# Choosing two experts with VectorE's eight-largest search, with two accumulator sums and one weight step moved on TensorE

## What is computed

```python
g_logits = xt @ w_router_group + b_router_group            # 4 groups
grp = argmax(g_logits); g_w = softmax(g_logits)[grp]
e_logits = (xt @ w_router_expert + b_router_expert).reshape(N, 4, 8)[grp]
top_p, top_i = top_k(softmax(e_logits), 2)
gates = g_w * top_p / sum(top_p)
expert = grp * 8 + top_i
# each chosen expert e, for its tokens: (silu(gate) * up) @ w_down[e], gate, up = split(x @ w_gate_up[e])
out[token] += y * gate
```

## Time and profile before

| | us |
|---|---|
| median of 3 runs | 666.59 |
| lowest and highest | 665.27, 667.97 |
| profiled execution, its own time | 664.23 |
| its span in the profile | 662.4 |
| TensorE busy | 507.2 (77%) |
| VectorE busy | 235.0 (35%) |
| ScalarE busy | 181.7 (27%) |
| read from HBM | 236.50 MB, 359 GB/s over the span |

### The profile page before, as it was taken

The page is one execution under the profiler, slowest core; times in us unless marked ns, Lnnn a source line. Parts: engine busy times, 40 slices in busy tenths (PEclk is TensorE's granted clock), DMA queues, the critical chain, the costliest instruction groups (busy, mean ns, idle before and its releaser), DMA issues.

```text
span 662.4 us, 13304 instructions
## 1 busy us (share of the span) xinstructions
PE 507.2 (77%) x5802; PEld 370.9 (56%) x5802; DVE 235.0 (35%) x522; ACT 181.7 (27%) x399; POOL 20.8 (3%) x21
## 2 busy tenths in 40 slices
PE   3999999999999898885755864765586476558665
PEld 3988998789888655553433532343353234335433
DVE  3796897664644632321111221121121112112203
ACT  6559567264442112110100020010002101000203
POOL 2000111200000000000000000000000000000000
PEclk9999999999999999999877988798798879889978
DMA  8755834396579889999999999999999999999992
GB/s 348 294 187 190 319 145 162 135 398 240 189 278 368 341 350 426 427 447 429 428 425 428 431 433 445 433 433 430 427 427 433 430 439 442 430 410 429 428 414 103
DMA packets 15717, 238.09 MB, mean 359 GB/s; under 512 B 1728, under 2 KB 1856, under 8 KB 3008
## 3 DMA queue, kind: packets, MB, share of 16 engines
q1 hardware_dynamic: 15536, 237.03, 85.9%
q10 hardware_dynamic: 144, 0.52, 0.2%
HBM read 236.50 MB, written 1.05 MB: 359 GB/s over the span
## 4 chain that ended last, share of the span: by engine, by line
PE 48%; DMA 44%; DVE 3%; ACT 2%; issue 1%; another core or an unknown queue 1%; POOL 1%; SPq 0%; POOLq 0%; ACTq 0%; DVEq 0%
DMA ring<-in_w_expert 43%; PE psum L617 15%; PE psum L600 11%; PE psum L903 10%; PE psum L934 4%; DMA landing<-in_dense 1%; PE psum L774 1%; PE psum L751 1%; PE psum L583 1%; PE psum L862 1%; PE psum L927 1%; PE psum L875 1%; POOL stat L1344 1%; PE psum L646 1%
## 5 line engine op out<-in xcount | busy, mean ns | idle before, releaser
L903 PE MATMUL psum<-ring,xg 128*32 128x256 f32 x2048 | 153.4, 461 | 90.4 <-DMA ring<-in_w_expert 84.2
L903 PEld LDWEIGHTS psum<-ring,xg 128*32 128x32 f32 x2048 | 74.3, 131 | 157.0 <-DMA ring<-in_w_expert 90.0
L617 PE MATMUL psum<-split_w,split_act 128*128 128x512 f32 x432 | 101.9, 393 | 1.2 <-DVE res L1596 1.2
L617 PEld LDWEIGHTS psum<-split_w,split_act 128*128 128x128 f32 x432 | 80.3, 188 | 18.3 <-DVE res L1596 1.6
L1282 ACT ACTIVATE small<-psum 128x128 f32<-128x128 f32 x32 | 8.9, 278 | 283.0 <-PE psum L903 283.0
L1839 DVE SCALAR_TENSOR_TENSOR small<-small,psum 128x128 f32<-128x128 f32 x32 | 9.2, 288 | 203.1 <-ACT small L1282 203.1
L1408 DVE TENSOR_TENSOR split_w<-landing,split_w 128x2048 fp32r<-128x2048 f32 x29 | 66.2, 2289 | 30.9 <-ACT split_w L1079 30.8
L1079 ACT ACTIVATE split_w<-landing 128x2048 fp32r<-128x2048 f32 x30 | 57.3, 1915 | 49.3 <-PE psum L617 26.0
L600 PE MATMUL psum<-split_act,split_w 128*128 128x256 f32 x576 | 70.1, 284 | 0.9 <-DVE split_act L1421 0.9
L600 PEld LDWEIGHTS psum<-split_act,split_w 128*128 128x128 f32 x576 | 69.5, 192 | 1.7 <-DVE split_w L1442 1.3
L1850 DVE COPY ybuf<-psum 32x128 f32<-32x128 f32 x128 | 37.3, 291 | 75.5 <-PE psum L934 74.6
(11 more groups left out here) (184 smaller groups left out, 355.4 us busy)
## 6 DMA issues: line engine op xcount, KB each, us to landing
ring<-in_w_expert SPq DMA_DIRECT2D x20, 6144.0 KB, 48.2
ring<-in_w_expert SPq DMA_DIRECT2D x23, 2048.0 KB, 33.8
landing<-in_dense SPq DMA_DIRECT2D x30, 1024.0 KB, 5.5
ring<-in_w_expert SPq DMA_DIRECT2D x26, 1024.0 KB, 8.3
res<-in_x SPq DMA_DIRECT2D x2, 512.0 KB, 3.7
work<-in_mem SPq DMA_DIRECT2D x1, 1024.0 KB, 11.4
ybuf<-in_late SPq DMA_DIRECT2D x1, 512.0 KB, 14.1
after_routing<-in_norm_final SPq DMA_DIRECT2D x1, 512.0 KB, 10.7
```

The source lines that it names most:

```text
L617: i = mm(b, tokens_of(src[t], k0 + k, h), w[a][:, k, :], start=first and k == 0 and n == 0, stop=last and k == CT - 1 and n == 2)
L903: i = mm(half[SLOTS * strip:SLOTS * strip + SLOTS], xg[:, CT * part + k, SLOTS * j:SLOTS * j + SLOTS], w[:, k, :, P * strip:P * strip + P] ...
```

## The change

- choose(h) takes the eight largest of the groups' logits (`V.max`) and their positions (`V.max_index`), masks the other groups' experts, and does the same once over the 32 masked expert logits; the first two positions are compared with 0 to 31 in one operation, whose two rows are added into `picked`. The group logits are padded from 4 to 8 columns with a bias of -1e30, so that a routing matmul has 40 columns. ScalarE's second exponential waits for `expert_arg` and has 2 columns.
- first_slots goes; find_slots and slots_times_rstd, each over all 128 slots, stand in its place. Ahead of the gathered tokens the gates take five linked steps, where there were five and an unlinked one.
- On TensorE, weights 28 are used for half 1 between Tf1 and Tf2; route(0, 1) goes ahead of route(1, 0).
- open_sum(0, 1) and open_sum(1, 1) stand ahead of and behind the last matmul of rank1; group 0 has none any more.

```diff
@@ -76,7 +77,8 @@
                      ("b_ig", CT), ("lru_lambda", CT), ("conv_w", CONV * CT)):
     PARAMS[_name] = (sum(n for _, n in PARAMS.values()), _cols)
 N_PARAMS = sum(n for _, n in PARAMS.values())
-N_ROUTES = GROUPS + EXPERTS
+EIGHT = 8
+N_ROUTES = EIGHT + EXPERTS
 
 
 CONSTS = {}
@@ -147,8 +149,11 @@
 def lay_out_late(inputs):
 
 
-    router = np.concatenate([np.asarray(inputs["w_router_group"])[0], np.asarray(inputs["w_router_expert"])[0]], axis=1)
-    bias = np.concatenate([np.asarray(inputs["b_router_group"]), np.asarray(inputs["b_router_expert"])], axis=1)
+    router = np.zeros((D, N_ROUTES), np.float32)
+    bias = np.full((1, N_ROUTES), -BIG, np.float32)
+    for name, a, n in (("group", 0, GROUPS), ("expert", EIGHT, EXPERTS)):
+        router[:, a:a + n] = np.asarray(inputs[f"w_router_{name}"])[0]
+        bias[:, a:a + n] = np.asarray(inputs[f"b_router_{name}"])
     blocks = np.zeros((P, 2, CT, P), np.float32)
     for n, name in enumerate(("w_rg", "w_ig")):
         w = np.asarray(inputs[name])[0]
...
@@ -803,16 +808,16 @@
             for c in (0, 1):
                 await_read(pe, f"xo{c}")
             turn("Tf", res, (0, 1))
+            tokens(28, ["xo2", "xo3"], os_, 0, last=False, halves=(1,))
             await_read(pe, "xo2")
             turn_late("Tf2", 0, range(CT, KC))
             pe.wait_ge(router_loaded, 16)
             for c in (0, 1):
                 await_read(pe, f"Tf{c}")
             route(0, 0)
-            route(1, 0)
             await_read(pe, "Tf2")
             route(0, 1)
-            tokens(28, ["xo2", "xo3"], os_, 0, last=False, halves=(1,))
+            route(1, 0)
             tokens(29, ["xo2", "xo3"], os_, CT, first=False, halves=(1,))
 
             picked = rt(4)
@@ -842,8 +847,11 @@
             pe.wait_ge(first_taken, 1)
             for part in range(2):
                 gather_first(0, part, range(CT))
+            pe.wait_ge(late_sumsq, 2 * NH)
+            open_sum(0, 1)
             pe.wait_ge(chosen, 2)
             end(mm(pb("rank1")[:, 0:EXPERTS], const("before"), picked[:, 1], start=False, stop=True), "rank1")
+            open_sum(1, 1)
             def count_all():
 
                 for h in range(NH):
...
@@ -978,14 +986,9 @@
                 for h in range(NH):
                     await_read(pe, f"route{h}")
                 gate_up(0, 0, 0, rest_and_count)
-                pe.wait_ge(late_sumsq, 2 * NH)
-                open_sum(0, 1)
                 await_read(pe, "over")
                 finish_expert(0, 0, 0)
-                gate_up(0, 1, 0)
-                open_sum(1, 1)
-                finish_expert(0, 1, 0)
-                for j in range(2, BATCH):
+                for j in range(1, BATCH):
                     expert(0, j, 0)
                 for cb in range(2):
                     scatter(0, cb, range(NH))
...
@@ -1271,8 +1274,8 @@
             release(i, "Tf3")
             act.wait_ge(group_arg, 2)
             nc.scalar.activation(rt(9, GROUPS), rt(8, GROUPS), ACT.Exp).then_inc(group_exp, 1)
-            act.wait_ge(chosen, 2)
-            nc.scalar.activation(soft[:, 32:40], soft[:, 24:32], ACT.Exp).then_inc(expert_exp, 1)
+            act.wait_ge(expert_arg, 2)
+            nc.scalar.activation(soft[:, 32:34], soft[:, 24:26], ACT.Exp).then_inc(expert_exp, 1)
...
@@ -1686,58 +1689,36 @@
             late_mean(0)
 
             def by_group(ap):
...
-            def first_of_max(*searches):
-
-                def operate(stage, src, best, cand, index, pick):
...
+                return ap.rearrange("p (g e) -> p g e", g=GROUPS)
+
+            def eights(n):
+                return small[:, 960 + 16 * n:976 + 16 * n].rearrange("p (h n) -> p h n", h=NH)
+
+            g_sum, less, e21 = soft[:, 52:54], soft[:, 24:26], soft[:, 32:34]
+            gate12 = soft[:, 36:40].rearrange("p (h n) -> p h n", h=NH)
+            g_best, g_index, best, index = eights(0), eights(1).bitcast(U32), eights(2), eights(3).bitcast(U32)
+            other = rt(10, GROUPS)
+            pick12 = small[:, 384:512].rearrange("p (h n e) -> p h n e", h=NH, n=2)
+            picked, masked = rt(4), rt(5)
 
             def choose(h):
 
-                t = slice(h, h + 1)
                 take_logits(h)
-                first_of_max((by_group(e_logit[:, t]), best1[:, t], cand[:, t], index[:, t], pick1[:, t]),
-                             (g_logit[:, t], g_best[:, t], g_cand[:, t], g_index[:, t], g_pick[:, t]))
-                V.tensor_tensor(rt(8, GROUPS)[:, t], g_logit[:, t], spread(g_best[:, t], g_logit[:, t]), ALU.subtract
+                g_logit, e_logit = logit[:, h, 0:EIGHT], by_group(logit[:, h, EIGHT:])
+                link(V.max(g_best[:, h], g_logit))
+                link(V.max_index(g_index[:, h], g_best[:, h], g_logit))
+                link(V.tensor_tensor(other[:, h], iota[:, 0:GROUPS], g_index[:, h, 0:1].to_broadcast([P, GROUPS]), ALU.not_equal))
+                link(V.scalar_tensor_tensor(by_group(masked[:, h]),
+                                            other[:, h].unsqueeze(2).to_broadcast([P, GROUPS, PER_GROUP]), -BIG, e_logit,
+                                            ALU.mult, ALU.add))
+                link(V.max(best[:, h], masked[:, h]))
+                link(V.max_index(index[:, h], best[:, h], masked[:, h]))
+                link(V.tensor_tensor(pick12[:, h], iota[:, 0:EXPERTS].unsqueeze(1).to_broadcast([P, 2, EXPERTS]),
+                                     index[:, h, 0:2].unsqueeze(2).to_broadcast([P, 2, EXPERTS]), ALU.is_equal))
+                V.tensor_tensor(picked[:, h], pick12[:, h, 0], pick12[:, h, 1], ALU.add).then_inc(chosen, 1)
+                V.tensor_tensor(rt(8, GROUPS)[:, h], g_logit[:, 0:GROUPS], g_best[:, h, 0:1].to_broadcast([P, GROUPS]), ALU.subtract
                                 ).then_inc(group_arg, 1)
-                link(V.scalar_tensor_tensor(rt(5)[:, t], rt(2)[:, t], -BIG, e_logit[:, t], ALU.mult, ALU.add))
-                first_of_max((rest[:, t], best2[:, t], cand[:, t], index[:, t], pick2[:, t]))
-                V.tensor_tensor(less[:, t], best2[:, t], best1[:, t], ALU.subtract)
-                link(V.tensor_tensor(picked[:, t], pick1[:, t], pick2[:, t], ALU.add))
-                V.tensor_tensor(picked[:, t], picked[:, t], spread(g_pick[:, t], picked[:, t]), ALU.mult).then_inc(chosen, 1)
+                V.tensor_tensor(less[:, h:h + 1], best[:, h, 1:2], best[:, h, 0:1], ALU.subtract).then_inc(expert_arg, 1)
                 dve.wait_ge(chosen, h + 1)
 
             def place(h):
@@ -1769,24 +1750,18 @@
                     i = slots_times_rstd(h)
                 i.then_inc(taken, 1)
 
-            def first_slots(h):
-
-                for e in range(BATCH):
-                    i = V.tensor_scalar(ntake[:, h, SLOTS * e:SLOTS * e + SLOTS], iota[:, 1:SLOTS + 1],
-                                        rankm[:, h, e:e + 1], stat[:, RS + 6 + h:RS + 7 + h], ALU.is_equal, ALU.mult)
-                return i
-
             choose(0)
             add_xo("xo3", 1, 1)
             late_tokens("Tf4", 6, 2, 1)
             late_mean(1)
             place(0)
-            first_slots(0).then_inc(first_taken, 1)
-            find_slots(0, 0)
+            link(find_slots(0, 0))
+            slots_times_rstd(0).then_inc(first_taken, 1)
             choose(1)
             place(1)
-            first_slots(1).then_inc(taken, 1)
             find_slots(1, 0).then_inc(slots_found, 1)
+            dve.wait_ge(slots_found, 1)
+            slots_times_rstd(1).then_inc(taken, 1)
 
             def give_gates(g):
 
@@ -1813,14 +1788,12 @@
             dve.wait_ge(group_exp, 1)
             link(V.tensor_reduce(g_sum, rt(9, GROUPS), AX.X, ALU.add))
             dve.wait_ge(expert_exp, 1)
-            link(V.scalar_tensor_tensor(gate1, e21, 1.0, spread(g_sum, gate1), ALU.add, ALU.mult))
-            link(V.reciprocal(gate1, gate1))
-            link(V.tensor_tensor(gate1, gate1, g_pick, ALU.mult))
-            link(V.tensor_tensor(e21, e21, gate1, ALU.mult))
-            V.tensor_tensor(pick1, pick1, spread(gate1, pick1), ALU.mult)
+            link(V.scalar_tensor_tensor(g_sum, e21, 1.0, g_sum, ALU.add, ALU.mult))
+            link(V.reciprocal(gate12[:, :, 0], g_sum))
+            link(V.tensor_tensor(gate12[:, :, 1], gate12[:, :, 0], e21, ALU.mult))
+            link(V.tensor_tensor(pick12, pick12, gate12.unsqueeze(3).to_broadcast([P, NH, 2, EXPERTS]), ALU.mult))
             take_gathered(0, 0)
-            link(V.tensor_tensor(pick2, pick2, spread(e21, pick2), ALU.mult))
-            link(V.tensor_tensor(by_group(gates), pick1, pick2, ALU.add))
+            link(V.tensor_tensor(gates, pick12[:, :, 0], pick12[:, :, 1], ALU.add))
             dve.wait_ge(slots_found, 1)
             give_gates(0)
             take_gathered(0, 1)
```

More of the change, by code:

```diff
@@ L20 @@
 I32 = mybir.dt.int32
+U32 = mybir.dt.uint32
 ALU = mybir.AluOpType
@@ L329, in rt @@
```

(4 more changed lines are left out.)

## The result

| | us |
|---|---|
| changed kernel, median of 6 runs | 660.81 (659.99 to 661.90) |
| before, median of 6 runs beside them | 666.11 (665.27 to 667.97) |
| ratio | 0.9933, 95% interval [0.9912, 0.9953] |
| a second set, 8 runs against 31 of before | 0.9952, [0.9931, 0.9973] |
| profiled execution | 660.75, span 658.9 |

The changed kernel is faster by the ratio, by 4.5 us (3.1 to 5.9) in the first set and 3.2 us (1.8 to 4.6) in the second; 2.9 us was forecast. The ratio is not the quotient of the medians: these lie 5.3 us apart in the first set and 2.4 us (664.36 and 661.94) in the second. The two profiled executions are 3.48 us apart.

What follows compares the result with a forecast made beforehand. The weight stream bounds the kernel, its end hanging on when the ring's refill begins. The terms 0.66 + 0.52 + 0.37 + 0.46 + 0.89 = 2.90 us give 666.59 - 2.9 = 663.7 us; range 661.6 to 666.2.

Steps and rivals of the forecast that it cites:

- the prediction's own condition: Weight stream: a sooner end of expert 0's first gate_up half brings the end sooner if the stream is emptied by then.
- (1): TensorE, weights 28's second half ahead of Tf2 and routing: gain 0.66 us; unit 3's earlier load alone gives nothing.
- (2): VectorE's slots of half 0, find_slots and one multiply: only 0.15 us gained, take_logits(1) at 224.5.
- (3): VectorE's search: choose(1) takes 2.15 us instead of 3.45, a search 0.25, `chosen` at 226.7.
- (4): Sums in TensorE's waits: open_sum(0,1) takes 0.94 us, rank1 at 227.6 instead of 228.75, 0.87 of choose(1)'s saving unused.
- (5): VectorE's slots of half 1: 0.37 us less, gather at 228.9, gain 1.55 us so far.
- (6): TensorE's clock does not drop: gate_up begins at 230.8 (0.46 us more), takes 1.93, not 2.82 (0.89 more).
- (7): Router: 40 columns instead of 36, the larger table and the smaller exponential cost nothing.
- A: Rival: TensorE's clock drops all the same, gain only 1.7 us, 664.9; chance 0.16.
- B: Rival: both holes of the weight stream close, the stream never waits, gain 4.3 us, 662.3; chance 0.12.
- C: Rival: VectorE's searches are expensive; at 1.14 us a search the kernel is 0.5% slower, 670; chance 0.04.
- D: Rival: the change does not reach the end, stream's rate or tail moves by as much, 666.6; chance 0.12.

Runs made afterwards that it cites:

- refill_sides: Changed kernel with the very first refill cut into two halves, the first issued when 16 of the 32 matmuls are done; ratio to before 0.9969.
- best: Changed kernel with open_sum(0, 1) directly behind rank1, open_sum(1, 1) in group 0, and the first refill in two halves; ratio to before 0.9968.
- search_more1: Changed kernel with the expert search done twice in each choose; one execution, no ratio, rank1 0.1 us and refill 0.2 us later.
- sums_in_group: Changed kernel with both accumulator sums back in group 0; one execution, no ratio, rank1 0.4 us and refill 0.31 us sooner.
- search_only: Kernel before with only VectorE's search, slots and gates changed, plus the 40 columns and ScalarE's wait; ratio to before 0.9966.
- search_more4: Changed kernel with the expert search repeated four times in each choose; one execution, no ratio, rank1 2.48 us and refill 3.66 us later.
- w28_only: Kernel before with only weights 28's second token half moved ahead of Tf2 and the routing; ratio to before 0.9978.

## Why the prediction was right, point by point

- **The bound.** That the end follows the first refill held in every trace but refill_sides and best: from refill to last wait 403.9 to 404.6 us, while the refill moved over a span of 4.0 us. In those two it is 405.7 and 405.2. In best the stream was still filling the ring when the refill was asked for, which the prediction's own condition excludes. In refill_sides it was not, the hole was there at 281 GB/s, and the step fails for a reason that no run shows.
- **(1)** 0.66 forecast; 0.75 alone, 0.78 in the changed kernel. That the early unit 3 gives nothing by itself was right.
- **(2), (3)** choose(1) took 2.17 us from take_logits at 224.53 to `picked` at 226.70 (forecast 2.15, 224.5 to 226.7). A search on 32 columns took 0.23 for the largest and 0.30 for the positions, hand-over included. The positions are two instructions in the trace, MATCH_VALUE_LOAD with 0.092 us and FIND_INDEX8 with 0.186. The Trainium skill has them as two (VectorE: DVE Perf Modes, "Two Vector instructions with no wait between them"), and the trace agrees. The load is about half of the 0.15 to 0.19 that the 2.4 us of that estimate had for it.
- **(4)** rank1 at 227.19, forecast 227.6. The mis-sized term is TensorE's: the gather began at 224.47 and a following matmul starts before the last one's modelled end (the sum at 226.33, the gather's end 226.50), so the sum was through 0.4 sooner, and choose(1) had 0.49 us to spare, not 0.87. So rank1 was 1.57 us sooner from the mark, not 1.18. search_more1 agrees with that margin, and sums_in_group shows that the sum is on the path.
- **(5), (6)** Gather at 228.50 (forecast 228.9), gate_up at 230.67 (230.8), 1.93 us for it. Between the gather and gate_up 0.17 us was gained, not 0.46. The gathered tokens were taken at 229.76 (forecast 230.05), 0.34 us after VectorE was free, because they wait for TensorE's gather. From there to gate_up it was 0.91 us, as before (231.90 to 232.81); the prediction had 0.75 there without a reason, and with 0.91 its own moments give 230.96.
- **(7)** held: the 24 routing matmuls of 40 columns took 2.76 us, the 24 of 36 columns 2.84.
- **The sum**: 2.90 forecast, 3.02 in both traces of the changed kernel. That it comes within 0.12 us is in part luck: rank1 gained 0.39 more than forecast and the step from the gather to gate_up 0.29 less. The slots (0.41 against 0.37) and the clock in gate_up (0.89) were right.
- **The rivals.** A did not happen. The clock held at 1.00 in search_only with 0.27, 1.00 and 0.56 us idle, and fell in search_more4 with 1.51 us idle in a stretch of 1.93 busy of 3.5. The Trainium skill's warning (TensorE: Matmul & The Clock Gate, "A second HAM failure mode: psum-queue depth-cycling") would have the clock swing with short, frequent idling. The traces here have it both ways: not with the idle times of search_only, but with the longer one of search_more4. B was not reached by the changed kernel; best, with both holes closed, gained nothing over it. C did not happen, and its sum was near: at 2.1 us more per choose it has the refill 0.4 us later than before the change (1.23 + 0.70 + 1.35 - 2.90), and search_more4 had it 0.6 later. D did not happen: the rate stayed at 431 GB/s, and the tail moved by 0.23 us.
- **The chances** had within 0.5% as the likeliest at 0.65. The ratio 0.9933 lies outside that, 0.9952 just inside, the traces' 3.0 to 3.5 us at the border. So the first set fell into what had 0.32, faster by more than 0.5%, and the 2.9 us of the forecast lie just below its interval (3.1 to 5.9). The median of 660.81 is 0.8 below the range's lower end of 661.6, and 2.9 below the 663.7. 666.59 x 0.9933 would be 662.1: of the miss 1.6 us is the first set's larger gain, 0.5 that the runs of before came out lower than the first three (666.11 against 666.59), and 0.8 that the ratio and the quotient of the medians (0.9920) differ.

Left open: why the first set gained 1.4 us more than the refill moved (its interval begins at 3.1), what makes the first 96 matmuls take 11.9 us in some executions and 13.4 to 13.9 in others, with the granted clock at 1.00 in both traces of the changed kernel, and why a first refill in two halves did not bring the end forward.

## What to carry to other kernels

When a saturated transfer stream ends the kernel, find the one request that starts it and count a change in microseconds at that request; freeing a unit earlier brings only what the stream doesn't idle away later. Work put into an engine's wait costs something as soon as the wait is shortened by the same change; put it behind what the wait was for. Where either of two edits would keep TensorE's clock up, the gain of the clock counts once.

## What the runs showed of the hardware that I had not expected

- Two matmul steps of 1 us each, moved ahead of and behind rank1 where TensorE had idled 1.48 and 1.31 us, were worth 1.1 us: the 32 matmuls took 2.82 and 2.95 us (before, w28_only) with the clock at the lower of its two levels (1.2 GHz) in their first part, and 1.93 with it at the upper throughout.
- FIND_INDEX8 on 32 columns took 0.186 us and MAX8 0.194, much the same as a reduction of 32 columns (0.187).
- The mark, with the same work ahead of it, came between 194.67 and 197.79 us over thirteen executions, as much as the whole gain: one execution's time can't judge such a change; distances within the trace repeated to 0.01 us at the refill and 0.24 us at the last wait.
